# Token-wise sums of squares, a diagonal product that spreads rstd, and a reordered first stage in a fused gMLP, attention and FFN kernel

## The chip, the cores and the metric

The kernel runs on 1 core of one Trainium2 chip. The metric is the device time in microseconds (us) of one execution. Engines are named as the profile names them: PE is TensorE (PEld its weight loads), DVE is VectorE, ACT is ScalarE, POOL is GpSimd, SP is SyncE; a q behind a name is the engine's own instruction stream, which also issues DMAs.

## The reference, cut to what matters

The program computes two blocks on x of 512 tokens by 1024 features: a gated MLP layer, a dilated attention layer with a shared KV projection, then a second block with two SwiGLU layers around a hybrid mixer. The change is in the first layer's start, and in a helper that two later norms use:

```
def ada_mod(c, w, b, n):
    h = jax.nn.silu(c) @ w + b
    return jnp.split(h[:, None, :], n, axis=-1)

def gmlp_layer(...):
    shift, scale, gate = ada_mod(c, ada_w, ada_b, 3)
    h = rms_norm(x, norm_g) * (1 + scale) + shift
    u, v, z = jnp.split(h @ w_in, 3, axis=-1)
    u = jax.nn.gelu(u)
    v = rms_norm(jax.nn.gelu(v), sgu_g)
...
def shared_kv(...):   # and dilated_layer, each with its own shift, scale and norm_g
    shift, scale = ada_mod(c, ada_w, ada_b, 2)
    h = rms_norm(x, norm_g) * (1 + scale) + shift
    k, v = jnp.split(h @ w_kv, 2, axis=-1)
```

rms_norm divides each token by the root of its mean square over the 1024 features; shift and scale are one number per feature. The matrix a_ada_w is 1024 x 3072 (shift, scale, gate), the v part of w_in is 1024 x 2048.

## The kernel before, in words

Activations lie transposed (features on partitions, tokens along the row): `xT` holds 8 tiles (`KD` = 8) of 128 features x 512 tokens. Every large product is made of three passes with operands split into a rounded high part and a low remainder. ACT makes the high part by a copy, DVE the low part by a subtraction. Weights come in chunks of 128 x 2048 numbers into the two slots of `raw` (SP issues the DMAs, `chunk_half` for the v part); `high_part(q, s, ...)` on ACT and `low_part(q, s)` on DVE split slot s of pair q; the low part's end raises `w_ready`, on which PE waits in `chunk` and SP in `wait_slot` before it fills a slot again.

All order is written by hand: each engine runs its own stream, and semaphores tie the streams. The first stage goes as follows.

- SP loads c and x (`xin`, 4 DMAs, token-major), waits for the sixth tile of a_ada_w (`ada0_landed[0]` at 32), then loads the first weight pair, `wsp`, `relrow` and the spatial bias. POOL loads the 8 tiles of a_ada_w (1 MB each, shift and scale columns) into five buffers `ada0_w`; ACT's queue loads 21 small rows (biases and norm gains, tables A and B, and the convolution's taps, `conv_dw_w`, last).
- PE waits for all the rows and transposes them into `sc[0]`, then turns x, 4 transposes for each `xT` tile, and between them sums the squares of finished tiles with a ones matrix into `misc` (`sum_square`), which gives every partition the sum for each token.
- ACT copies each turned tile to `xT` and squares it. DVE adds up c times a_ada_w in `ada0_acc` (`ada0_tile`, one a_ada_w tile at a time, the eighth in halves), with the column copies after the third tile, and `reciprocal_root(0)` (mean square, ACT's root, a reciprocal over 128 x 512) between the sixth and the seventh.
- PE sums `ada0_acc` over partitions (`ada_sum`, 8 one-column products for shift and 8 for scale). DVE adds the bias (`ada_columns`), forms (1 + scale) g (`scale_columns`), and `apply` makes the 8 tiles of h: a multiply by scale and `rstd`, an add of shift, then the low part after ACT's high part (`high_of`).
- `v_block(b)`, b = 0 to 3, multiplies h by 512 columns of v: 8 tiles of h x 4 token blocks x 3 passes = 96 passes of 512 columns, into `v_bank`; the first four tiles use slot 0, the last four slot 1. ACT takes the banks out with Gelu, and `v_block(b + 1)` waits for that. Between blocks 0 and 1 PE transposes `wsp`, which ACT copies to `wsT`.

`apply` runs again after the output product of the layer ("ao"): for the KV norm all eight tiles in one go, and for the attention norm two tiles at a time inside the KV loop (`m` < 4). There the order on DVE is, for each m, `next_low`, `kv_after` (two reciprocals for the k norm), then `apply` of two tiles; ACT's `next_high` for the next chunk stands behind the high parts of those tiles. The loops of "ao" on ACT and DVE are register loops (`Fori`).

## Time and profile before

| | |
|---|---|
| median of 3 runs | 2167.16 us (2163.77 to 2168.45) |
| profiled execution, its own time | 2169.68 us |
| its span | 2168.1 us |
| instructions | 23510 |
| PE busy | 1988.6 us, 92% |
| DVE busy | 1139.0 us, 53% |
| ACT busy | 795.1 us, 37% |
| DMA | 198.40 MB, mean 92 GB/s |

The profiled execution's time is 1.6 us more than its span, and 2.5 us above the median. A busy PE is not a PE at its peak, since the clock granted to it can be 1.2 or 2.4 GHz (0.50 or 1.00 in the profile).

### The profile page before, as it was taken

What the parts mean: (1) busy time and instruction counts of PE and PEld (TensorE: products, weight loads), DVE (VectorE), ACT (ScalarE), POOL (GpSimd) and SP (SyncE); (2) the same over time, 40 slices, a digit from 0 to 9 for tenths busy, and PEclk for the clock granted to TensorE, in tenths of its full rate; (3) what the DMA queues carried; (4) which work ended last, traced back from release to release, by engine and by line L of the source; (5) the groups of instructions that cost most, each with busy time, mean ns of one, the idle gap of its engine ahead of it and who ended that gap; (6) DMA issues with size and microseconds to landing.
All of it is one profiled execution on the core that took longest, in us unless ns stands there. A gap on an engine that the chain in (4) does not pass through costs nothing.

```text
span 2168.1 us, 23510 instructions
## 1 busy us (share of the span) xinstructions
PE 1988.6 (92%) x8658; PEld 1570.8 (72%) x8658; DVE 1139.0 (53%) x1408; ACT 795.1 (37%) x995; POOL 38.6 (2%) x95
## 2 busy tenths in 40 slices
PE   3899999989999999799999996899996989999997
PEld 2688888867777777478888884686664757888885
DVE  4436656468344454454433456399744555433455
ACT  2336554233355444332222233223334343222232
POOL 1000000000000000000000000000000000000000
PEclk9899999979999999899999998999998999999998
DMA  6345555412212121023333322232210223334321
GB/s 256 127 142 158 167 173 164 144 55 75 74 42 59 39 59 39 20 83 96 91 96 101 97 82 73 78 112 64 59 46 32 78 58 97 92 88 112 97 73 63
DMA packets 288193, 198.40 MB, mean 92 GB/s; under 512 B 6562, under 2 KB 275188, under 8 KB 287092
## 3 DMA queue, kind: packets, MB, share of 16 engines
q1 hardware_dynamic: 279568, 163.63, 26.3%
q0 software_dynamic: 8064, 33.56, 4.4%
q8 instruction: 52, 0.85, 0.2%
q10 hardware_dynamic: 484, 0.16, 0.0%
q14 instruction: 25, 0.20, 0.0%
HBM read 195.21 MB, written 2.11 MB: 91 GB/s over the span
## 4 chain that ended last, share of the span: by engine, by line
PE 82%; DVE 10%; ACT 4%; issue 3%; DMA 1%; ACTq 0%; DVEq 0%
PE acc L563 19%; PE acc L565 19%; PE acc L564 19%; PE acc L738 3%; PE acc L740 3%; PE acc L739 3%; PE ob L796 2%; PE sc L755 2%; DVE s_rstd L1426 1%; ACT s_w_high L1004 1%; PE acc L946 1%; PE acc L948 1%; PE acc L947 1%; PE ob L779 1%; DMA s_rows<-in_conv_dw_w 1%
## 5 line engine op out<-in xcount | busy, mean ns | idle before, releaser
L1388 DVE TENSOR_TENSOR s_w_low<-s_raw,s_w_high 128x2048 fp32r<-128x2048 f32 x160 | 366.7, 2292 | 360.4 <-ACT s_w_high L1004 360.1
L563 PE MATMUL acc<-s_h_high,s_w_high 128*128 128x512 f32 x1248 | 492.9, 395 | 32.3 <-DVE s_h_low L1747 12.2
L565 PE MATMUL acc<-s_h_high,s_w_low 128*128 128x512 f32 x1248 | 486.5, 390 | 0.0
L564 PE MATMUL acc<-s_h_low,s_w_high 128*128 128x512 f32 x1248 | 486.5, 390 | 0.0
L1004 ACT ACTIVATE s_w_high<-s_raw 128x2048 fp32r<-128x2048 f32 x160 | 305.1, 1907 | 28.0 <-PE sc L642 19.3
L563 PEld LDWEIGHTS acc<-s_h_high,s_w_high 128*128 128x128 f32 x1248 | 234.8, 188 | 91.5 <-issue 35.2
L563 PE MATMUL acc<-s_b_high,s_w_high 128*128 128x512 f32 x640 | 257.9, 403 | 33.3 <-DVE s_branch L1938 15.9
L565 PEld LDWEIGHTS acc<-s_h_high,s_w_low 128*128 128x128 f32 x1248 | 234.7, 188 | 49.0
L564 PEld LDWEIGHTS acc<-s_h_low,s_w_high 128*128 128x128 f32 x1248 | 235.0, 188 | 48.6 <-issue 1.4
L565 PE MATMUL acc<-s_b_high,s_w_low 128*128 128x512 f32 x640 | 253.5, 396 | 0.0
L564 PE MATMUL acc<-s_b_low,s_w_high 128*128 128x512 f32 x640 | 253.4, 396 | 0.0
L563 PEld LDWEIGHTS acc<-s_b_high,s_w_high 128*128 128x128 f32 x640 | 122.9, 192 | 67.0 <-DVE s_branch L1938 17.6
L564 PEld LDWEIGHTS acc<-s_b_low,s_w_high 128*128 128x128 f32 x640 | 123.2, 193 | 26.0 <-issue 1.0
L565 PEld LDWEIGHTS acc<-s_b_high,s_w_low 128*128 128x128 f32 x640 | 122.7, 192 | 26.2
L1770 DVE TENSOR_TENSOR s_hd<-s_rstd,acc 128x512 f32<-128x512 f32 x44 | 30.2, 687 | 166.4 <-PE acc L565 166.4
L738 PE MATMUL acc<-s_h_high,s_w_high 128*128 128x512 f32 x256 | 113.4, 443 | 0.8 <-DVE s_v L1634 0.8
L1027 ACT ACTIVATE s_b_high<-s_hd 128x512 f32 (+1 forms) x44 | 27.8, 632 | 208.4 <-DVE s_hd L1773 208.4
L740 PE MATMUL acc<-s_h_high,s_w_low 128*128 128x512 f32 x256 | 103.6, 405 | 0.0
L739 PE MATMUL acc<-s_h_low,s_w_high 128*128 128x512 f32 x256 | 103.6, 405 | 0.0
L1839 DVE SCALAR_TENSOR_TENSOR s_cy<-s_glu,s_cols,s_cy 128x512 f32<-128x512 f32 x120 | 81.3, 745 | 0.0
L1240 ACT ACTIVATE s_sg<-s_sg 128x512 f32<-128x512 f32 x44 | 27.8, 632 | 133.8 <-DVE s_sg L1768 133.8
L1684 DVE SCALAR_TENSOR_TENSOR s_s_row<-sc,s_tiny,s_bias 128x256 f32<-128x256 f32 (+3 forms) x96 | 43.7, 511 | 55.7 <-PE sc L755 32.7
(257 smaller groups left out, 2323.5 us busy)
## 6 DMA issues: line engine op xcount, KB each, us to landing
s_raw<-in_a_w_in SPq DMA_DIRECT2D x48, 512.0 KB, 5.0
s_raw<-in_ffn_w_gate SPq DMA_DIRECT2D x44, 512.0 KB, 4.0
s_raw<-in_ffn_w_up SPq DMA_DIRECT2D x44, 512.0 KB, 5.2
s_raw<-in_w_in SPq DMA_DIRECT2D x36, 512.0 KB, 4.4
s_raw<-in_b_w_in SPq DMA_DIRECT2D x32, 512.0 KB, 4.9
s_ada_w<-in_b_ada_w POOLq DMA_DIRECT2D x24, 512.0 KB, 5.0
s_raw<-in_ffn_w_down SPq DMA_DIRECT2D x32, 384.0 KB, 4.2
s_raw<-in_ffn_w_down SPq DMA_DIRECT2D x32, 320.0 KB, 3.7
```

Of the source, the lines that this page charges most:

```text
L563: pe.matmul(acc[b][:, :], w_high[:, o:o + P], hi, start=(k == 0), stop=False, skip_group_check=grouped)
L564: pe.matmul(acc[b][:, :], w_high[:, o:o + P], lo, start=False, stop=False, skip_group_check=grouped)
L565: mm = pe.matmul(acc[b][:, :], w_low[:, o:o + P], hi, start=False, stop=(k == nk - 1), skip_group_check=grouped)
L738: pe.matmul(acc[b][:, :], w_high[:, o:o + P], hi, start=(k == 0), stop=False, skip_group_check=True)
L739: pe.matmul(acc[b][:, :], w_high[:, o:o + P], lo, start=False, stop=False, skip_group_check=True)
L740: mm = pe.matmul(acc[b][:, :], w_low[:, o:o + P], hi, start=False, stop=(k == KD - 1), skip_group_check=True)
L755: mm = pe.matmul(sc[g][:, DIST_W[g] - w:DIST_W[g]], qT[j][g][:, qt * P:(qt + 1) * P], kT[:, k + (qt + 1) * P - w:k + (qt + 1) * P], start= ...
L796: mm = pe.matmul(ob[:, k * P:end * P], v1[:, v:v + P], pT[:, src:src + (end - k) * P], start=(n == 0), stop=(n == len(order) - 1), skip_gr ...
L1004: act.activation(w_high[:, s * SLOT:(s + 1) * SLOT], raw[:, s * SLOT:(s + 1) * SLOT], ACT.Copy)\
L1388: dve.tensor_tensor(w_low[:, w], raw[:, w], w_high[:, w].bitcast(F32), ALU.subtract).then_inc(w_ready, 1)
L1684: ins = dve.scalar_tensor_tensor(out=s_row[b][:, at_:at_ + w], in0=sc[g][:, DIST_W[g] - w:DIST_W[g]], scalar=tiny[:, qr:qr + 1], in1=bias[ ...
L1839: dve.scalar_tensor_tensor(out=cy_n, in0=seg(glu, i + n * GW, T), scalar=col("conv_dw_w_2", i * CT + n), in1=cy_n, op0=ALU.mult, op1=ALU.a ...
```

## The change

The sums of squares of the first norm are no longer made from the turned tiles. ACT squares the token-major `xin` and accumulates along the row, so each token (partition) gets its own sum in a column of `tiny`; the root and the reciprocal are of 128 x 4 numbers. DVE multiplies the identity by these four columns (`diag`, 128 x 512), and one product of a ones matrix with `diag` puts rstd of every token on every partition, in `misc`; `apply` reads it there. PE turns x before it turns any rows, and only table A's rows; table B's and the taps are turned after `v_block(0)`, and `wsp` after `v_block(1)`. DVE runs six a_ada_w tiles in a row. The last tile's halves run scale first, and its sum goes ahead. Twelve products without use (`WARM`) stand on PE behind the sixth a_ada_w tile. The first weight slot is split in quarters, its low parts between the tiles of `apply`, and the second slot's behind the sixth tile. In `apply` with a shift, the add of the shift moves into ACT's high part (Identity with a bias) and into DVE's subtraction; `n2` goes. A Gelu of four numbers stands on ACT ahead of the block loop, and `high_part` of a block's second slot comes ahead of the squares of v. The "ao" loops on ACT and DVE are unrolled. SP's first weights wait for the seventh a_ada_w tile; rows, `wsp` and `relrow` lie elsewhere in memory, and POOL waits for `rel_stored` before its later loads.

```diff
+WARM = 12
...
+        x_sq_out = [at(f"x_sq_out{j}", o, D) for j, o in enumerate((TMP + 2 * TILE, HH))]
+        diag = at("diag", TMP + TILE, T)
         rstd = at("rstd", TMP + TILE, T)
         sq = [at(f"sq{j}", TMP + (2 + j) * TILE, T) for j in range(2)]
         n1 = [at(f"n1{j}", TMP + (4 + j) * TILE, T) for j in range(2)]
-        n2 = [at(f"n2{j}", TMP + (6 + j) * TILE, T) for j in range(2)]
...
-            sp.wait_ge(ada0_landed[0], 32)
+            sp.wait_ge(ada0_landed[1], 32)
...
+            pool.wait_ge(rel_stored, 16)
...
-            pe.wait_ge(rows_landed, 16 * ROW_DMAS)
-            pe.wait_ge(c_ready, 1)
-            for j, n in enumerate(ROW_COUNTS):
-                mm = pe.transpose(sc[0][:, j * P:j * P + n], rows[j][0:n, :], ident[0:n, 0:n])
-            mm.then_inc(rows_turned, 1)
...
-                if k >= 2:
-                    sum_square(0, k - 2)
-            sum_square(0, KD - 2)
-            sum_square(0, KD - 1)
-            for b in range(2):
-                pe.wait_ge(ada0_used, KD + b)
-                ada_sum(ada0_acc, b, b * D)
+            pe.wait_ge(rows_landed, 16 * len(ROWS_A))
+            pe.wait_ge(c_ready, 1)
+            pe.transpose(sc[0][:, 0:ROW_COUNTS[0]], rows[0][0:ROW_COUNTS[0], :], ident[0:ROW_COUNTS[0], 0:ROW_COUNTS[0]])\
+                .then_inc(rows_turned, 1)
+
+            pe.wait_ge(ada0_used, KD - 2)
+            for k in range(WARM):
+                pe.matmul(ob[:, 384:512], ident[:, :], ones[:, :], start=True, stop=True)
+            pe.wait_ge(diag_ready, 1)
+            pe.matmul(misc[:, :], ones[:, :], diag[:, :], start=True, stop=True).then_inc(spread_ready, 1)
+            for b in (1, 0):
+                pe.wait_ge(ada0_used, KD + 1 - b)
+                ada_sum(ada0_acc, b, b * D, (sc[0], ob)[b])
...
-                    chunk(2 * b + half)
+                    if b > 0 or half > 0:
+                        chunk(2 * b + half)
                     for kk in range(4):
                         k = 4 * half + kk
+                        if b == half == 0 and kk < 3:
+                            pe.wait_ge(first_low, kk + 1)
+                        elif b == half == 0:
+                            chunk(0)
...
+            pe.wait_ge(rows_b_landed, 16 * (len(ROWS_B) + 1))
+            pe.wait_ge(cols_ready, 1)
+            for j, n in enumerate(ROW_COUNTS):
+                if j > 0:
+                    mm = pe.transpose(sc[0][:, j * P:j * P + n], rows[j][0:n, :], ident[0:n, 0:n])
+            mm.then_inc(rows_b_turned, 1)
+            v_block(1)
             pe.wait_ge(wsp_ready, 1)
-            pe.wait_ge(cols_ready, 1)
+            pe.wait_ge(cols_b_ready, 1)
...
+                if shift is None:
+                    act.activation(seg(dst, k * T, T), src, ACT.Copy).then_inc(done, 1)
+                else:
+                    act.activation(seg(dst, k * T, T), src, ACT.Identity, bias=shift).then_inc(done, 1)
...
+            act.wait_ge(x_landed, 16 * TT)
             for k in range(KD):
                 act.wait_ge(x_turned, k + 1)
                 act.activation(xT[:, k * T:(k + 1) * T], xb[k % 3][:, :], ACT.Copy).then_inc(x_stored, 1)
-                act.wait_ge(x_stored, k + 1)
-                square(xT[:, k * T:(k + 1) * T], k % 2, 0, k)
-            root(0)
-            high_part(0, 0, 0)
+                if k % 2 == 0:
+                    t = k // 2
+                    if t >= 2:
+                        act.wait_ge(x_sq, t - 1)
+                    act.activation(x_sq_out[t % 2][:, :], xin[:, t * D:(t + 1) * D], ACT.Square,
+                                   accum_out=tiny[:, V_SS + t:V_SS + t + 1]).then_inc(x_sq, 1)
+            act.wait_ge(ms_ready, 1)
+            act.activation(tiny[:, V_RT:V_RT + 4], tiny[:, V_MS:V_MS + 4], ACT.Sqrt).then_inc(root_ready, 1)
+            act.wait_ge(w_landed[0], 32)
+            for k in range(4):
+                act.activation(w_high[:, k * T:(k + 1) * T], raw[:, k * T:(k + 1) * T], ACT.Copy)\
+                   .then_inc(first_high if k < 3 else w_high_ready, 1)
             for k in range(KD):
-                high_of(n2[k % 2][:, :], h_high, k, h32_ready, k + 1, h_high_ready)
+                high_of(n1[k % 2][:, :], h_high, k, h32_ready, k + 1, h_high_ready, shift=ada[:, SHIFT_A + k:SHIFT_A + k + 1])
+                if k == 3:
+                    high_part(0, 1, 0)
+            act.activation(tiny[:, V_MS:V_MS + 4], tiny[:, V_SS:V_SS + 4], ACT.Gelu_apprx_tanh)
             for b in range(4):
-                high_part(b, 1, 4 * b)
                 act.wait_ge(half_used, b + 1)
                 high_part(b + 1, 0, 0)
-                if b == 0:
+                if b == 1:
...
+                if b < 3:
+                    high_part(b + 1, 1, 4 * b + 4)
...
-            with act.Fori(0, 4) as i:
+            for i in range(4):
...
-                high_of(n2[k % 2][:, :], b_high, k, h32_ready, KD + k + 1, h_high_ready)
+                high_of(n1[k % 2][:, :], b_high, k, h32_ready, KD + k + 1, h_high_ready,
+                        shift=ada[:, SHIFT_KV + k:SHIFT_KV + k + 1])
...
+            def apply(hbase, scale, shift, high, low, tiles=range(KD), spread=None, between=None):
+
+                def low_tile(k):
+
+                    dve.wait_ge(h_high_ready, hbase + k + 1)
+                    low_k, high_k = low[:, k * T:(k + 1) * T], high[:, k * T:(k + 1) * T].bitcast(F32)
+                    if shift is None:
+                        dve.tensor_tensor(low_k, n1[k % 2][:, :], high_k, ALU.subtract).then_inc(h_ready, 1)
+                    else:
+                        dve.scalar_tensor_tensor(out=low_k, in0=n1[k % 2][:, :], scalar=shift(k), in1=high_k,
+                                                 op0=ALU.add, op1=ALU.subtract).then_inc(h_ready, 1)
 
                 for k in tiles:
-                    if k >= 2:
+                    if hbase + k >= 2:
                         dve.wait_ge(h_high_ready, hbase + k - 1)
                         dve.wait_ge(h_ready, hbase + k - 1)
-                    x_k = xT[:, k * T:(k + 1) * T]
-                    if shift is None:
-                        dve.scalar_tensor_tensor(out=n2[k % 2][:, :], in0=x_k, scalar=scale(k), in1=rstd[:, :],
-                                                 op0=ALU.mult, op1=ALU.mult).then_inc(h32_ready, 1)
-                    else:
-                        own.done(dve.scalar_tensor_tensor(out=n1[k % 2][:, :], in0=x_k, scalar=scale(k), in1=rstd[:, :],
-                                                          op0=ALU.mult, op1=ALU.mult))
-                        dve.tensor_scalar(n2[k % 2][:, :], n1[k % 2][:, :], shift(k), None, ALU.add).then_inc(h32_ready, 1)
+                    dve.scalar_tensor_tensor(out=n1[k % 2][:, :], in0=xT[:, k * T:(k + 1) * T], scalar=scale(k),
+                                             in1=(rstd if spread is None else spread)[:, :],
+                                             op0=ALU.mult, op1=ALU.mult).then_inc(h32_ready, 1)
+                    if between is not None:
+                        between(k)
                     if k > tiles[0]:
-                        low_of(n2[(k - 1) % 2][:, :], high, low, k - 1, h_high_ready, hbase + k, h_ready)
-                k = tiles[-1]
-                low_of(n2[k % 2][:, :], high, low, k, h_high_ready, hbase + k + 1, h_ready)
-
-            def ada_columns(n0, n1_, read):
+                        low_tile(k - 1)
+                low_tile(tiles[-1])
...
-            for k in range(3):
+            for k in range(6):
                 ada0_tile(k)
+            dve.wait_ge(x_sq, TT)
+            dve.tensor_scalar(tiny[:, V_MS:V_MS + 4], tiny[:, V_SS:V_SS + 4], 1.0 / D, EPS, ALU.mult, ALU.add).then_inc(ms_ready, 1)
+            ada0_tile(6)
+            dve.wait_ge(root_ready, 1)
+            dve.reciprocal(tiny[:, V_R:V_R + 4], tiny[:, V_RT:V_RT + 4]).then_inc(x_rcp, 1)
+            dve.wait_ge(x_rcp, 1)
+            dve.tensor_tensor(diag[:, :].rearrange("p (t q) -> p t q", t=TT),
+                              ident[:, None, :].broadcast_to([P, TT, P]),
+                              tiny[:, V_R:V_R + 4].rearrange("p (t q) -> p t q", q=1).broadcast_to([P, TT, P]),
+                              ALU.mult).then_inc(diag_ready, 1)
             dve.wait_ge(rows_turned, 1)
-            for j, n in enumerate(ROW_COUNTS):
-                ins = dve.tensor_copy(cols[:, j * P:j * P + n], sc[0][:, j * P:j * P + n])
-            ins.then_inc(cols_ready, 1)
+            dve.tensor_copy(cols[:, 0:ROW_COUNTS[0]], sc[0][:, 0:ROW_COUNTS[0]]).then_inc(cols_ready, 1)
             dve.wait_ge(cols_ready, 1)
-
+            for half in (1, 0):
+                ada0_tile(7, half)
+            ada_columns(8, 16, 1)
+            dve.wait_ge(ada_cols, 1)
+            scale_columns(A_A, SHIFT_A + KD, "a_norm_g")
+            ada_columns(0, 8, 2, sc[0])
+            dve.wait_ge(ada_cols, 2)
+            dve.wait_ge(spread_ready, 1)
+
+            def first_lows(k):
+
+                if k < 4:
+                    part = slice(k * T, (k + 1) * T)
+                    if k < 3:
+                        dve.wait_ge(first_high, k + 1)
+                    else:
+                        dve.wait_ge(w_high_ready, 1)
+                    dve.tensor_tensor(w_low[:, part], raw[:, part], w_high[:, part].bitcast(F32), ALU.subtract)\
+                       .then_inc(first_low if k < 3 else w_ready, 1)
+                elif k == 5:
+                    low_part(0, 1)
+
+            apply(0, lambda k: derived_col(A_A + k), lambda k: ada_col(SHIFT_A + k), h_high, h_low,
+                  spread=misc, between=first_lows)
...
-            for k in range(3, 6):
-                ada0_tile(k)
-            reciprocal_root(0)
-            ada0_tile(6)
-            for half in range(2):
-                ada0_tile(7, half)
-            low_part(0, 0)
-            ada_columns(0, 16, 2)
-            dve.wait_ge(ada_cols, 1)
-            scale_columns(A_A, SHIFT_A + KD, "a_norm_g")
-            apply(0, lambda k: derived_col(A_A + k), lambda k: ada_col(SHIFT_A + k), h_high, h_low)
...
+                if b == 0:
+                    dve.wait_ge(rows_b_turned, 1)
+                    for j, n in enumerate(ROW_COUNTS):
+                        if j > 0:
+                            ins = dve.tensor_copy(cols[:, j * P:j * P + n], sc[0][:, j * P:j * P + n])
+                    ins.then_inc(cols_b_ready, 1)
+                    dve.wait_ge(cols_b_ready, 1)
+                    for dst, name in ((HG1, "ffn1_norm_post_2"), (HG2, "ffn2_norm_post_2")):```

The order is shown at three places. First DVE, from its first instruction to the first tile of `apply`. Before (`s_ada_acc` is `ada0_acc`, `s_ada_w_77` to `81` its five buffers):

```order
L1474 SCALAR_TENSOR_TENSOR s_ada_acc<-s_ada_w_79,s_tiny,s_ada_acc 128x2048
L1481 COPY s_cols<-sc 128x106
L1481 COPY s_cols<-sc 128x84
L1481 COPY s_cols<-sc 128x124
L1485 SCALAR_TENSOR_TENSOR s_derived<-s_cols 128x1
L1488 TENSOR_SCALAR s_derived<-s_cols 128x8 x2
L1474 SCALAR_TENSOR_TENSOR s_ada_acc<-s_ada_w_80,s_tiny,s_ada_acc 128x2048
L1474 SCALAR_TENSOR_TENSOR s_ada_acc<-s_ada_w_81,s_tiny,s_ada_acc 128x2048
L1474 SCALAR_TENSOR_TENSOR s_ada_acc<-s_ada_w_77,s_tiny,s_ada_acc 128x2048
L1418 TENSOR_SCALAR s_n_68<-misc 128x512
L1426 RECIPROCAL s_rstd<-s_n_69 128x512
L1474 SCALAR_TENSOR_TENSOR s_ada_acc<-s_ada_w_78,s_tiny,s_ada_acc 128x2048
```

Of the change, the same stretch on DVE, from the sixth a_ada_w tile to the first tile of `apply`:

```order
L1519 SCALAR_TENSOR_TENSOR s_ada_acc<-s_ada_w_78,s_tiny,s_ada_acc 128x2048
L1525 TENSOR_SCALAR s_tiny<-s_tiny 128x4
L1519 SCALAR_TENSOR_TENSOR s_ada_acc<-s_ada_w_79,s_tiny,s_ada_acc 128x2048
L1528 RECIPROCAL s_tiny<-s_tiny 128x4
L1530 TENSOR_TENSOR s_diag<-s_ident,s_tiny 128x512
L1535 COPY s_cols<-sc 128x106
L1519 SCALAR_TENSOR_TENSOR s_ada_acc<-s_ada_w_80,s_tiny,s_ada_acc 128x1024 x2
L1495 TENSOR_TENSOR s_ada<-ob,s_cols 128x8
L1498 SCALAR_TENSOR_TENSOR s_derived<-s_ada,s_cols 128x8
L1495 TENSOR_TENSOR s_ada<-sc,s_cols 128x8
L1483 SCALAR_TENSOR_TENSOR s_n_71<-s_xT,s_derived,misc 128x512
```

The copy of the columns stands behind the seventh tile instead of the third, and the reciprocal is of 4 columns. Second, PE of the change around the end of `v_block(0)` (L651, L653 and L655 are its passes, `s_rows_86` and `87` the late rows):

```order
L651 MATMUL sc<-s_w_high,s_h_high 128x512
L653 MATMUL sc<-s_w_low,s_h_high 128x512
L655 MATMUL sc<-s_w_high,s_h_low 128x512
L667 MATMUL sc<-s_ident,s_rows_86 128x84
L667 MATMUL sc<-s_ident,s_rows_87 128x124
L651 MATMUL acc<-s_w_high,s_h_high 128x512
```

Where these two transposes stand there were eight of `wsp` before (L653 of the kernel before). Third, ACT of the change, from the last high part of h to the second block's copies of `wsT`:

```order
L1050 ACTIVATE s_h_high<-s_n_72,s_ada 128x512
L1089 ACT_TABLE_LOAD
L1089 ACTIVATE s_tiny<-s_tiny 128x4
L1024 ACTIVATE s_w_high<-s_raw 128x2048
L1100 ACTIVATE s_v_tok<-acc 128x4x128 x2
L1100 ACTIVATE s_v_tok<-sc 128x4x128 x2
L1024 ACTIVATE s_w_high<-s_raw 128x2048
L1109 ACTIVATE s_sq_69,s_tiny<-s_v_tok 128x512
```

The Gelu's table load stands ahead of block 0's end; before, it stood behind the copies of `wsT`, directly ahead of the first Gelu. POOL gains one wait, and SP's DMAs keep their order.

## Rows read from the trace of the kernel before

**Rows 1.** The page: engine shares (part 1) and two groups of part 5.

```profile
PE 1988.6 (92%) x8658; PEld 1570.8 (72%) x8658; DVE 1139.0 (53%) x1408; ACT 795.1 (37%) x995; POOL 38.6 (2%) x95
...
L1388 DVE TENSOR_TENSOR s_w_low<-s_raw,s_w_high 128x2048 fp32r<-128x2048 f32 x160 | 366.7, 2292 | 360.4 <-ACT s_w_high L1004 360.1
```

**Rows 2.** The chain that ended last, 0 to 110 us: start, us, what.

```profile
8.85 20.04 DMA s_rows<-in_conv_dw_w
...
43.90 3.36 DVE s_rstd L1426
47.29 2.36 DVE s_ada_acc L1474
...
51.09 7.00 PE ob L596 x32
58.52 0.76 DVE s_n L1439
59.31 0.49 DVE s_n L1441
```

**Rows 3.** Timeline at 25 us: start, us, engine and line, [idle before <-releaser].

```profile
25.60 1.92 SPq L358 DMA_DIRECT2D s_raw<-in_a_w_in  x4
```

**Rows 4.** DMA issues in windows at 3.0, 12, 17 and 26 us: KB, us to landing.

```profile
s_xin<-in_x SPq DMA_DIRECT2D x1, 512.0 KB, 12.3
...
s_ada_w<-in_a_ada_w POOLq DMA_DIRECT2D x1, 1024.0 KB, 13.0
...
s_ada_w<-in_a_ada_w POOLq DMA_DIRECT2D x1, 1024.0 KB, 11.3
...
s_raw<-in_a_w_in SPq DMA_DIRECT2D x1, 512.0 KB, 7.6
```

**Rows 5.** Windows: us, busy PE, PEld, DVE, ACT, POOL, then PEclk, DMA share, GB/s.

```profile
61.70:74.30 12.60, 12.58 (x48) 9.98 (x48) 11.70 (x19) 4.58 (x7) 0.00 (x0) 0.88 0.01 2
77.69:90.34 12.65, 12.65 (x49) 10.20 (x49) 2.36 (x2) 1.92 (x1) 0.00 (x0) 0.87 0.55 178
458.30:471.50 13.20, 11.25 (x21) 6.16 (x22) 11.79 (x20) 5.16 (x7) 0.00 (x0) 0.50 0.00 1
1370.00:1374.00 4.00, 2.34 (x11) 1.65 (x10) 1.36 (x2) 2.49 (x2) 0.00 (x0) 1.00 0.85 230
1374.00:1377.00 3.00, 3.00 (x15) 2.47 (x14) 1.68 (x1) 0.00 (x0) 0.00 (x0) 1.00 0.05 10
```

**Rows 6.** Timeline of 61 to 120 us, blocks 0 and 1 of v.

```profile
61.72 0.77 PE L638 MATMUL acc<-s_w_high,s_h_high 128*128 128x512 f32 x1 [3.65 <-DVE s_h_low L1399]
...
77.69 0.50 PE L638 MATMUL acc<-s_w_high,s_h_high 128*128 128x512 f32 x1 [3.38 <-DVE s_w_low L1388]
...
78.51 33.63 SPq L358 DMA_DIRECT2D s_raw<-in_a_w_in  x9
...
92.51 1.28 ACT L1065 ACT_TABLE_LOAD   x1
...
94.55 0.47 PE L638 MATMUL acc<-s_w_high,s_h_high 128*128 128x512 f32 x1 [3.17 <-ACT s_v_tok L1065]
...
118.01 0.39 PE L638 MATMUL acc<-s_w_high,s_h_high 128*128 128x512 f32 x1
```

**Rows 7.** Timeline of PE at 161 us: one ada_sum of 8 columns.

```profile
161.53 1.84 PE L596 MATMUL ob<-s_ones,s_gate_acc 128*128 128x1 f32 x16
163.24 0.49 PE L563 MATMUL acc<-s_h_high,s_w_high 128*128 128x512 f32 x1
```

**Rows 8.** Timeline of 455 to 510 us: KV norm and KV loop.

```profile
455.13 0.75 DVE L1439 SCALAR_TENSOR_TENSOR s_n<-s_xT,s_derived,s_rstd 128x512 f32<-128x512 f32 x1
...
470.11 0.80 PE L563 MATMUL acc<-s_b_high,s_w_high 128*128 128x512 f32 x1 [0.33 <-DVE s_b_low L1399]
...
497.57 0.63 ACT L1027 ACTIVATE s_h_high<-s_n 128x512 fp32r<-128x512 f32 x1 [0.55 <-DVE s_n L1441]
...
509.09 0.76 PE L563 MATMUL acc<-s_b_high,s_w_high 128*128 128x512 f32 x1 [3.72 <-ACT s_k_sq L1113]
```

70 lines of the change are left out of this document (38 added, 32 removed).

## The prediction, made before the changed kernel ran

> **What bounds the kernel now.** I read the engine shares first: PE is busy for 92% of the span, DVE for 53% [rows 1]. A change that takes nothing off PE's products can only win where PE stands still or runs at its lower clock. So I went to the chain of the first 110 us, where PE's first large product starts only at 61.72 [rows 6]. Its first long link is a DMA: the taps of the convolution are issued at 8.85 and land 20.04 us later, and PE, which waits for all rows, turns nothing until 28.9 [rows 2]. The x that it could have turned landed at about 2.8 + 12.3 = 15.1 [rows 4]. Behind that the chain goes through turning x and summing squares to 42.5, the reciprocal over 128 x 512 (3.36), the seventh and eighth a_ada_w tiles and the one-column sums (7.00), until `apply` starts at 58.52 [rows 2]. The timeline then shows two more holes in PE: 3.38 us ahead of the second half of block 0, where the low part of slot 1 stands behind all eight tiles of h, and 3.17 ahead of block 1, behind the copies of `wsT`, a table load and the first Gelu [rows 6]. After each hole some passes run at 1.2 GHz: 48 passes took 12.6 us in both halves of block 0 at a mean granted clock of 0.88 and 0.87 [rows 5]. At full clock a pass takes 0.227 (the timeline's pitch; 96 passes from 94.55 to 118.01 are 23.46, less the passes at half clock below), so 48 are 10.9 and each ramp costs 1.7. Later, the KV norm feeds PE tile by tile from 455.13 to 470.11 [rows 8].
>
> **A. From the start to `apply`.** The waits for rows and for squares go; what is left is the pace of a_ada_w. Tile 6 is issued behind the first tile's use at 12.6 and lands at 12.6 + 13.0 = 25.6, when SP, waiting for it, issues its weights [rows 3, 4]. Each tile on DVE takes 2.36 [rows 2]: 28.0. The mean square of 128 x 4 is a small operation of about 0.2 (two of them lie between the end of the sums at 58.09 and 58.52 [rows 2]): 28.2. Tile 7 lands at 17.3 + 11.3 = 28.6 [rows 4] and is done at 30.9. The small reciprocal 0.2, `diag` 0.7 (DVE's operations on 512 columns cost 0.49 to 0.76 [rows 2]), the column copy 0.2: 32.0. Two halves at 1.3: 33.3 and 34.6. The scale sum runs from 33.3; eight columns take 1.71 at full clock [rows 7] and 3.5 at half (7.00 for sixteen [rows 2]). At full clock the two sums end at 35.0 and 36.8, and with the last small operations `apply` starts at 37.3 against 58.52: **21.2 us**. At half clock it is 40.9 and 17.6. [...]
>
> What lies beside it: ACT copies and squares x from 16 on, eight copies of 0.6 and four squares of 1024 columns, each half of a 2048-column copy (1.9) plus 0.2 for the accumulator, some 10 us, ended at 26; it is covered by DVE's tiles until 28.0. Without that cover each us counts in full. SP's first weights are issued at 28.6 instead of 25.6; the first slot then took until 26.1 + 7.6 = 33.7 [rows 4], now 36.7 at most. ACT's first quarter is ready at 37.4, DVE asks for it at 38.0. This is the thinnest cover: 0.6 us.
>
> **B. `apply` and block 0.** A tile had a period of 1.97 on DVE: 0.79 for the multiply, 0.40 for the shift, 0.78 for the low part. Now it is the multiply (reading rstd from PSUM, which I bound by the same 0.75, since the multiply-add of the residual reads PSUM at that price) and a low part of 0.75: 1.46. Four quarters of a low part add 0.6 each (2292 ns over four [rows 1]). The first tile is ready after two multiplies, two quarters and its low part, 3.3 us; before it was 3.2: **-0.1**. With quarters a tile takes 2.1, less than PE's 2.7 for twelve passes at full clock, so PE is not starved again. The low part of slot 1 is then done 11.8 us into `apply`, PE asks at 3.3 + 12.6 = 15.9: the hole of 3.38 goes, and with it the second ramp, 1.7: **5.1**.
>
> **C. Block 0 to block 1.** Block 0 ended at 90.34, block 1 began at 94.55, 4.21 later [rows 5, 6]. Now two short transposes, 0.3, and the Gelu of the first bank has its 2 us before the block ends: **3.9**, and no ramp in block 1: **1.7**. But the weights of block 1 must be there. DVE ends `apply` 16.3 after its start, then the small operations, 0.4, SP's next issue 0.7, 5.4 until landing (78.51 to 83.87), ACT 1.95, DVE 2.3: 27.1. PE is through with block 0 at 3.3 + 12.6 + 10.9 + 0.3 = 27.1. A tie; I charge nothing and keep 1 us for the range.
>
> **D. Block 1 to block 2.** The transposes of `wsp` move here: 1.0 for them, 1.1 for the two copies, 0.65 for the Gelu, 0.1 of waits: **-2.9**. PE is idle for 1.8 of it. A hole of 1.66 at 1370 us is like this (PE busy for 2.34 of 4.00), and the clock stayed at 1.00 in and behind it [rows 5], so I add no ramp (it would be 1.7).
> The load that B and C take from the path is priced by its row, 1.28, with the Gelu following at 93.81 [rows 6]. The Trainium skill, "ScalarE: Activation LUTs", What ACT_TABLE_LOAD costs, gives some 1.38 us of drain on top; by it the gain would be 1.4 more, 2133.1 on the runs' scale, inside the forecast's own range. The trace shows no such drain on this load.
>
> **E. The two later norms.** The KV norm's last tile was ready 14.95 after its first multiply (470.11 against 455.13 [rows 8]). At 1.46 a tile it is 11.8: **3.1**. In the KV loop the two high parts stand ahead of the weight's high part on ACT; the second began at 497.57 [rows 8], after the multiply and the shift of its tile. Without the shift it follows the first directly, 0.6 earlier, once before PE's hole of 3.72 at 509.09 [rows 8], behind which PE is busy: **0.6**. Unrolling the "ao" loops: 0.2 at the last tile's register waits, else hidden by PE.
>
> **Other edits at nothing:** table B's columns and the halved gains are made while DVE waits in block 1; the second slots' high parts go ahead of squares that nobody needs until block 3's end; POOL's new wait ends near 57, and its next loads wait for uses long after. Without these covers each is 0.2 to 2 us.
>
> **Sum:** 21.2 - 0.1 + 5.1 + 3.9 + 1.7 - 2.9 + 3.1 + 0.6 + 0.2 = 32.8. The v, "uz" and "ao" stages between are PE-bound without holes (none is listed from 118 to 446), so it is passed on. The profiled 2169.7 becomes 2136.9; the runs' median is 2.5 lower, so **2134.5**, I say 2135.
>
> **The rivals.**
> 1. *The sums run at 1.2 GHz, or the weights are late* (0.14). For it: the 32 one-column passes at 51 us ran at half clock to their end, 7.00 against twice 1.71 [rows 2, 7], and the cover of 0.6 at the first quarter is thin. Against: dense products go right ahead. 3.6 less, with a late quarter or a ramp in D of 1.7 more: 2138 to 2142.
> 2. *The gain of B and C comes back as a wait for weights* (0.05). If SP's second pair lands late, behind `wsp`, the spatial bias and POOL's four gate tiles, block 1 waits as it did: 10.6 less, 2145.
> 3. *PE is starved tile by tile and never gets its clock* (0.02). In the KV norm PE ran 13.2 us at 0.50 because each tile came alone, PE busy for 11.25 of it [rows 5]. If an operand in PSUM made a tile of `apply` dearer than PE's 2.7, block 0 would run at half clock, and if that lasted over 33 / 0.2 = 165 passes the gain would be gone; over all four blocks, 384 passes, it is 77 - 33 = 44 slower: 2211. Against: 2.1 is well under 2.7, and after block 0 h is all there.
> 4. *It does nothing* (0.01): if a_ada_w's tiles came later by what the rows were earlier. Against: their DMAs are issued by the same uses as before, 2167.
> 5. *More than the sum* (0.08): PE, fed every 1.46 with 1.28 of work at half clock, may get its clock inside the KV norm, 24 passes earlier at 0.2, some 2 to 5: 2130 to 2133.
>
> **How the numbers follow.** My forecast (0.70) is 2135 with 2131 to 2139 as its own range: half clock in one sum, 1 us in C, 1.7 in D, and the KV loop's other two savings of 0.6. Rival 5 reaches down to 2130; I take 2128, since the squares of x and the small operations are not in the trace. Upwards rival 1 reaches to 2142, and I take 2144 for both of its parts with a wait in C. That leaves out rivals 2 to 4 and a tenth beside. A measurement of this kernel tells 0.2%, some 4.3 us, from no change. Faster: all but rivals 3 and 4, 0.97; the same 0.01; slower 0.02.
>
> **What would show it.** In the changed kernel: PE's first transposes of x near 15 to 16; the last a_ada_w half ended near 34.6; each ada_sum 1.7 long; the first multiply of `apply` near 37 and PE's first pass of v near 41; no hole between the halves of block 0; a hole under 1 us ahead of block 1 and one of about 1.8 ahead of block 2, which starts near 89; the KV norm's tile period 1.46. Wrong would make it: ada_sums of 3.5, a first quarter that DVE waits for, a period over 2.7 in `apply`, or a later stage that has a new hole.

## The result, and the profile of the changed kernel

The changed kernel takes 2128.71 us (median of 4 runs, 2128.28 to 2132.92), the kernel before 2167.8 on the same chip (4 runs, 2163.77 to 2170.78). The ratio is 0.9834 with a 95% interval of 0.9820 to 0.9847: 1.5 to 1.8% faster. The medians differ by 39.1 us, the spans of the two profiled executions by 2168.1 - 2127.1 = 41.0. The forecast was 2135 with a gain of 32.8.

The page's engine shares answer to [rows 1]:

```profile
PE 1971.6 (93%) x8668; PEld 1563.1 (73%) x8668; DVE 1125.9 (53%) x1389; ACT 796.2 (37%) x999; POOL 38.8 (2%) x95
```

The chain that ended last (start, us, what) answers to [rows 2]:

```profile
12.65 12.95 DMA s_ada_w<-in_a_ada_w
25.62 2.36 DVE s_ada_acc L1519
28.02 5.26 PE ob L624 x24
33.28 0.86 PE misc L626 x2
34.15 1.68 PE ob L603 x16
35.83 2.85 PE sc L603 x16
38.97 0.75 DVE s_n L1483
```

The DMA of the taps is gone from the chain; the pace of a_ada_w is on it, as forecast. But what follows the sixth tile is not DVE's last two tiles. It is PE's own `WARM` products, 5.26 long, and the `diag` product and the two sums stand in line behind them. `apply` starts at 38.97, before at 58.52.

The timeline of all engines from 31 to 43 us shows both sides of that, and what came behind it (start, us, engine, line, [idle before <-releaser]):

```profile
31.86 2.48 DVE L1519 SCALAR_TENSOR_TENSOR s_ada_acc<-s_ada_w,s_tiny,s_ada_acc 128x1024 f32<-128x1024 f32 x2
...
33.98 1.84 PE L603 MATMUL ob<-s_ones,s_ada_acc 128*128 128x1 f32 x16
35.69 2.98 PE L603 MATMUL sc<-s_ones,s_ada_acc 128*128 128x1 f32 x16
...
39.96 1.32 POOL L508 TENSOR_SCALAR_AFFINE_SELECT s_wsp<-s_wsp 128x1024 f32<-128x1024 f32 x1 [19.44 <-DMA s_wsp<-in_a_w_spatial]
...
40.90 0.92 DVE L1554 TENSOR_TENSOR s_w_low<-s_raw,s_w_high 128x512 fp32r<-128x512 f32 x1
...
42.63 0.77 PE L651 MATMUL acc<-s_w_high,s_h_high 128*128 128x512 f32 x1 [3.96 <-DVE s_h_low L1476]
```

DVE ended at 34.34, within 0.3 of the forecast. The first sum ran in 1.84, the second needed 2.98. A low part of a weight quarter took 0.92 where its neighbours take 0.68, in the very microsecond in which POOL masks `wsp`.

Windows (us, busy PE, PEld, DVE, ACT, POOL, PEclk, DMA share, GB/s) show the granted clock in that stretch, and below it the stretches of block 0, block 1 and the KV norm; they answer to [rows 5]:

```profile
30.00:32.00 2.00, 2.00 (x11) 2.00 (x11) 1.93 (x5) 0.00 (x0) 0.00 (x0) 0.50 0.91 326
...
34.00:35.00 1.00, 1.00 (x11) 1.00 (x10) 0.34 (x1) 1.00 (x3) 0.00 (x0) 1.00 0.91 301
...
37.00:38.00 1.00, 1.00 (x6) 1.00 (x6) 0.00 (x0) 0.00 (x0) 0.00 (x0) 0.50 1.16 355
...
42.63:66.36 23.73, 23.73 (x96) 19.40 (x97) 15.09 (x19) 11.13 (x13) 0.71 (x2) 0.92 0.49 178
66.70:88.30 21.60, 21.60 (x97) 17.85 (x96) 7.32 (x8) 6.62 (x11) 1.06 (x2) 1.00 0.57 195
...
433.00:435.00 2.00, 2.00 (x5) 1.22 (x5) 1.90 (x3) 0.72 (x1) 0.00 (x0) 0.50 0.00 0
435.00:437.00 2.00, 1.89 (x6) 0.81 (x4) 1.90 (x4) 0.96 (x2) 0.00 (x0) 0.83 0.00 0
437.00:440.00 3.00, 1.93 (x6) 0.97 (x6) 2.79 (x5) 1.41 (x3) 0.00 (x0) 1.00 0.00 0
```

PE was busy without a gap from 30 to 38, yet its clock was at 1.2 GHz, then 2.4, then 1.2 again. Block 0 is one piece now, 96 passes in 23.73 (before 28.62 from 61.72 to 90.34), with one ramp; block 1 has none. In the KV norm the clock comes back at about 435.7; before it stayed at 0.50 to the end of that stretch.

The timeline of PE at two later places answers to [rows 6, 8]:

```profile
91.18 0.47 PE L651 MATMUL acc<-s_w_high,s_h_high 128*128 128x512 f32 x1 [1.75 <-ACT s_v_tok L1100]
...
477.09 0.77 PE L570 MATMUL acc<-s_b_high,s_w_high 128*128 128x512 f32 x1 [3.08 <-ACT s_k_sq L1151]
```

Block 2 starts 26.8 us earlier than before (118.01) and the hole in the KV loop is 0.64 shorter (3.72).

**Where the 41.0 us come from.** I paired PE's instructions of the two traces and read by how much each starts earlier: 26.8 at block 2, 27.1 at the sum of squares ahead of the KV norm, 32.7 at the pass that stood at 535.69, 34.4 at the first scores, 38.4 at the first product of "bo", 40.9 at the end. So some 8 us appear in places that the change does not touch. The experiments below show what these are, as far as they do.

### The profile page after: what moved, and what is told of

It is laid out like the page before. It is cut to its first block, busy times and chain, and to the rows that moved or that the text cites. A ratio compares the mean times of both kernels' runs of the same rounds, so it can differ in the third digit from the quotient of the medians.

```text
span 2127.1 us, 23436 instructions
## 1 busy us (share of the span) xinstructions
PE 1971.6 (93%) x8668; PEld 1563.1 (73%) x8668; DVE 1125.9 (53%) x1389; ACT 796.2 (37%) x999; POOL 38.8 (2%) x95
## 4 chain that ended last, share of the span: by engine, by line
PE 84%; DVE 8%; ACT 4%; issue 3%; DMA 1%; DVEq 0%; POOL 0%; ACTq 0%; POOLq 0%
PE acc L570 20%; PE acc L571 19%; PE acc L572 19%; PE acc L758 3%; PE acc L760 3%; PE acc L759 3%; PE ob L816 2%; PE sc L775 2%; DVE s_rstd L1465 1%; PE acc L966 1%; DMA s_ada_w<-in_a_ada_w 1%; ACT s_w_high L1024 1%; PE ob L799 1%; PE acc L968 1%; PE acc L967 1%
## 5 line engine op out<-in xcount | busy, mean ns | idle before, releaser
L1427 DVE TENSOR_TENSOR s_w_low<-s_raw,s_w_high 128x2048 fp32r<-128x2048 f32 x159 | 364.5, 2292 | 354.0 <-ACT s_w_high L1024 354.0
L570 PE MATMUL acc<-s_h_high,s_w_high 128*128 128x512 f32 x1248 | 494.0, 396 | 31.5 <-DVE s_h_low L1820 11.5
L1024 ACT ACTIVATE s_w_high<-s_raw 128x2048 fp32r<-128x2048 f32 x159 | 303.3, 1907 | 23.7 <-PE sc L655 18.0
L570 PEld LDWEIGHTS acc<-s_h_high,s_w_high 128*128 128x128 f32 x1248 | 235.0, 188 | 89.8 <-issue 36.2
L570 PE MATMUL acc<-s_b_high,s_w_high 128*128 128x512 f32 x640 | 255.9, 400 | 30.4 <-DVE s_branch L2011 15.4
L570 PEld LDWEIGHTS acc<-s_b_high,s_w_high 128*128 128x128 f32 x640 | 121.9, 190 | 62.8 <-DVE s_branch L2011 17.4
## 6 DMA issues: line engine op xcount, KB each, us to landing
s_raw<-in_a_w_in SPq DMA_DIRECT2D x48, 512.0 KB, 5.1
s_raw<-in_ffn_w_gate SPq DMA_DIRECT2D x44, 512.0 KB, 4.0
s_raw<-in_ffn_w_up SPq DMA_DIRECT2D x44, 512.0 KB, 5.2
s_raw<-in_w_in SPq DMA_DIRECT2D x36, 512.0 KB, 4.2
s_raw<-in_b_w_in SPq DMA_DIRECT2D x32, 512.0 KB, 4.9
s_ada_w<-in_b_ada_w POOLq DMA_DIRECT2D x24, 512.0 KB, 5.0
```

Of the source, the lines that this page charges most:

```text
L570: pe.matmul(acc[b][:, :], w_high[:, o:o + P], hi, start=(k == 0), stop=False, skip_group_check=grouped)
L1024: act.activation(w_high[:, s * SLOT:(s + 1) * SLOT], raw[:, s * SLOT:(s + 1) * SLOT], ACT.Copy)\
L1427: dve.tensor_tensor(w_low[:, w], raw[:, w], w_high[:, w].bitcast(F32), ALU.subtract).then_inc(w_ready, 1)
```

## Both kernels again

> The kernel before, again, for its spread. In the first profiles the changed kernel ran 55 passes of 512 columns at half clock outside the parts that the change touches, the kernel before 75, and 8.3 us of the 41.0 between the two profiles stand there. Theory P (the clock's dips fall by chance in time): this second profile of the same code shows another number of slow passes, 55 to 90, and places in the attention stage that moved; the total lies within 2163 to 2172. Rival C (the change carries it): the same dips at the same places, 75 again within 3.

> The changed kernel, again. Theory P: its slow passes outside the touched parts vary too, 50 to 85, and the gain at the start of the third v block stays 26.8 within 0.5, while the gain at the end differs from 40.9 by some us. Rival C: 55 within 3 and 40.9 within 1.

The kernel before took 2166.74 (10 runs) beside 2165.74 of its reference runs, ratio 1.0006 (0.9996 to 1.0015), span 2163.6. The changed kernel took 2132.04 (4 runs, 2128.79 to 2132.98), ratio 0.9849 (0.9825 to 0.9873), span 2127.1: 33.7 by these medians.

By these second profiles the gain at the end is 2163.6 - 2127.1 = 36.5 in place of 41.0, as theory P has it. One thing that I expected did not come: the gain at block 2 did not stay within 0.5 of 26.8. It is 27.4 (117.71 against 90.31), because `apply` started 1.6 earlier in this profile of the changed kernel than in the first.

Windows over two stretches tell the four profiled executions apart: from the sum ahead of the KV norm to the first scores, and the attention stage (to "bo"). First the kernel before, its first profile:

```profile
449.20:579.00 129.80, 116.85 (x474) 90.31 (x475) 86.73 (x91) 46.63 (x63) 4.49 (x7) 0.88 0.22 65
579.00:916.80 337.80, 310.73 (x1430) 237.53 (x1428) 161.72 (x294) 159.32 (x257) 0.00 (x0) 0.95 0.16 44
```

Its second profile:

```profile
449.00:579.00 130.00, 117.89 (x474) 91.35 (x475) 86.74 (x91) 45.95 (x63) 4.49 (x7) 0.87 0.23 65
579.00:912.80 333.80, 306.87 (x1430) 234.54 (x1428) 161.43 (x294) 159.67 (x256) 0.00 (x0) 0.96 0.16 45
```

The changed kernel:

```profile
422.10:544.70 122.60, 112.09 (x475) 87.37 (x476) 79.94 (x75) 47.12 (x63) 4.44 (x7) 0.93 0.24 69
544.70:878.30 333.60, 306.42 (x1429) 234.44 (x1427) 161.57 (x294) 159.69 (x257) 0.00 (x0) 0.96 0.16 45
```

The attention stage of one and the same kernel took 337.8 and 333.8. The 4 us are PE's own busy time, 310.7 against 306.9 for the same 1430 records, at a lower mean clock. The changed kernel has 333.7 in both profiles. So 4.1 of the 41.0 is how the clock fell in the first profile of before, and not the change.

The first stretch, up to each profile's own first score, took 129.8 and 130.3 in the two profiles of before, 122.6 and 121.5 in those of the changed kernel: 7 to 9 us less, where I had forecast 3.9. Not all of it is the change's. These are the last 8 us ahead of the first scores, in the kernel before, in the changed kernel, and in the changed kernel with its copies of `wsT` moved, an edit far from this stage (`e12_wst_timed`, below):

```profile
571.00:579.00 8.00, 8.00 (x33) 6.62 (x34) 1.35 (x3) 4.39 (x7) 0.00 (x0) 0.79 0.50 133
...
536.70:544.70 8.00, 8.00 (x48) 7.02 (x48) 2.69 (x3) 4.20 (x8) 0.00 (x0) 1.00 0.49 132
...
535.40:543.40 8.00, 8.00 (x34) 6.59 (x34) 1.29 (x3) 4.06 (x7) 0.00 (x0) 0.79 0.48 131
```

PE is busy throughout in all three, but in the first and the third the clock is lower, and there the work from the pass that stood at 535.69 to the first scores takes 43.2 to 43.3, in the changed kernel 41.6. That is 1.6 us. This dip stands in six of all fourteen profiles, three of them of variants of the changed kernel. Over the ten profiles of the changed kernel and its variants the whole stretch took 121.5 to 124.5, so it gained 5.3 to 8.8.

## The two parts apart: the fold of the shift, and the order of the first stage

The fold alone, on the kernel before:

```diff
-high_of(n2[k % 2][:, :], h_high, k, h32_ready, k + 1, h_high_ready)
+high_of(n1[k % 2][:, :], h_high, k, h32_ready, k + 1, h_high_ready, shift=ada[:, SHIFT_A + k:SHIFT_A + k + 1])
...
+                        dve.scalar_tensor_tensor(out=low_k, in0=n1[k % 2][:, :], scalar=shift(k), in1=high_k,
+                                                 op0=ALU.add, op1=ALU.subtract).then_inc(h_ready, 1)
```

> The kernel before with one part of the change alone: the shift folded into ACT's high part and DVE's subtraction, in all three norms with a shift. My theory: the tile period in the KV norm falls from 1.97 to 1.52 (3.2 over the eight tiles), the KV loop gives 0.7, and the first apply ends 3 us earlier, which lets the second half of block 0 start 3 earlier: 6 to 7 in all, and up to 3 more if the clock comes back inside the KV norm: 2158 to 2162. Rival: the part matters only in the KV stage, where it gave 5.5 in the changed kernel's profile, clock included: 2162 to 2164.

The order alone, on the kernel before (ones-matrix sums of squares kept, x turned ahead of the rows, the column copies behind the eighth tile):

```diff
             for k in range(KD):   # x turned, squares summed
...
             sum_square(0, KD - 1)
+            pe.wait_ge(rows_landed, 16 * ROW_DMAS)
+            pe.wait_ge(c_ready, 1)
+            for j, n in enumerate(ROW_COUNTS):
+                mm = pe.transpose(sc[0][:, j * P:j * P + n], rows[j][0:n, :], ident[0:n, 0:n])
+            mm.then_inc(rows_turned, 1)
```

> The kernel before with the order alone changed: x turned and squared ahead of the rows, DVE's column copies behind the eighth a_ada_w tile; the sums of squares by turned tiles, the reciprocal over 128 x 512 and the rest stay. My theory: the first apply starts at 28.0 + 4.8 (mean square, root, reciprocal) + 2 x 2.4 + 1.2 + 7.0 behind the eighth tile's first half, near 44 to 45, 14 earlier than 58.5, and the time is 2153 to 2155. Rival: the wait for the taps was nearly all of it and the cheaper root is a trifle: 19 to 20 earlier, 2148.

The fold alone took 2152.69 (5 runs, 2149.85 to 2156.68), ratio 0.9949 (0.9928 to 0.9969). That is 13.1 below its reference of 2165.74, and more than I expected. Its timeline of PE:

```profile
60.42 0.77 PE L637 MATMUL acc<-s_w_high,s_h_high 128*128 128x512 f32 x1 [2.89 <-DVE s_h_low L1441]
...
89.38 0.47 PE L637 MATMUL acc<-s_w_high,s_h_high 128*128 128x512 f32 x1 [3.17 <-ACT s_v_tok L1067]
```

Block 0's first pass is 1.3 earlier and block 1 is 5.2 earlier than in [rows 6], with no hole inside block 0: eight tiles at 0.5 less each bring the low part of slot 1 forward by 4, which is more than the 3.38 that PE waited for it. Of the 5.2, 0.5 is that `apply` itself happened to start earlier, at 57.98. The rest of the gain comes later: its stretch from the sum to the first scores took 120.8, before 129.8 and 130.3, so that gain needs none of the other edits.

The order alone took 2150.24 (5 runs, 2147.06 to 2153.95), ratio 0.9931 (0.9909 to 0.9953), 15.5 below the reference and somewhat below the 2153 to 2155 that I expected. Its timelines, of DVE and PE:

```profile
43.94 0.75 DVE L1439 SCALAR_TENSOR_TENSOR s_n<-s_xT,s_derived,s_rstd 128x512 f32<-128x512 f32 x1
...
63.12 0.50 PE L638 MATMUL acc<-s_w_high,s_h_high 128*128 128x512 f32 x1 [2.64 <-DVE s_w_low L1388]
```

`apply` starts 14.6 earlier, the holes remain, and the KV stretch takes 130.4 as before. So of the 19.6 to 21.1 us ahead of `apply`, 14.6 come from not waiting for the rows. The other 5 to 6.5 belong to the rest of the change: the token-wise sums with the small root, the scale sum ahead, and the warming products. Of these only the warming products were tried by themselves (below). The gains of the two parts, 13.1 and 15.5, add up to 28.6, most of the 33.7; a kernel with both and nothing else was not run.

## The warming products

```diff
-WARM = 12
+WARM = 0
```

(In the second kernel `+WARM = 8`; these products have no use in the result.)

> The changed kernel without the twelve products that have no use. Theory W (they raise the clock, but stand in the way): without them the diag product runs at half clock as soon as diag is ready, 31.7 to 33.4, both column sums run at half clock, 3.5 each, and the first apply starts near 40.8 instead of 38.97, 1.8 later. Rival: the products only delay, the sums' speed comes from the turning of x: apply starts near 37.3, 1.7 earlier.

> The changed kernel with eight of these products instead of twelve. In the changed kernel they took 5.26 us at half clock, and the diag product, ready to start at 31.6, started at 33.1. Theory W: with eight they end at 31.5, the diag product is done by 33.4, the sums start with the first half of the last tile at 33.2, at full clock, and apply starts at 37.3 to 38.0, 1.0 to 1.7 earlier. Rival: with less dense work the clock does not rise and apply starts near 40.8, as without any.

Without them, 2136.89 in one run. Its timeline of PE:

```profile
31.86 2.05 PE L626 MATMUL misc<-s_diag,s_ones 128*128 128x512 f32 x2 [9.20 <-DVE s_diag L1530]
33.70 3.41 PE L603 MATMUL ob<-s_ones,s_ada_acc 128*128 128x1 f32 x16
36.97 3.55 PE L603 MATMUL sc<-s_ones,s_ada_acc 128*128 128x1 f32 x16
```

Both sums run at half clock, `apply` starts at 40.83, as worked out for the rival. With eight, 2128.45:

```profile
28.04 3.78 PE L624 MATMUL ob<-s_ones,s_ident 128*128 128x128 f32 x16 [5.93 <-DVE s_ada_acc L1519]
31.80 1.53 PE L626 MATMUL misc<-s_diag,s_ones 128*128 128x512 f32 x2
33.30 1.95 PE L603 MATMUL ob<-s_ones,s_ada_acc 128*128 128x1 f32 x16
35.10 2.70 PE L603 MATMUL sc<-s_ones,s_ada_acc 128*128 128x1 f32 x16
```

Here `diag` is waited for, not PE, and the scale sum starts at 33.30, when DVE has it ready; `apply` starts at 38.11. In the changed kernel's second profile the clock rose sooner, the twelve products took 4.29, the two sums 1.95 and 1.93, and `apply` started at 37.40. So the products bring the start of `apply` forward by 1.9 to 3.4 us, against a single profile without them, and block 2, which stands at 93.15 there, by 2.0 to 2.8. In six profiles with twelve of them that can be compared `apply` started between 37.24 and 38.97, in three with eight between 37.78 and 38.11: twelve cost some of their gain again when the clock rises late. Whether and where the clock falls again inside the second sum differs from run to run. At block 2 hardly anything of the difference was left in this run (91.08 against 91.18), in part because a low part of a weight quarter took 1.50 beside POOL's masking.

## The masking of the spatial weights

In the changed kernel's second profile the low part of the first tile of h took 1.58 instead of 0.74, while POOL masked `wsp`. Theory: the two operations get in each other's way. The experiment puts the masking behind `apply`:

```diff
-            pool.wait_ge(wsp_landed, 16)
-            pool.affine_select(out=wsp[:, :].rearrange("t (g s) -> t g s", g=AG),
...
             for k in range(KD):
+                if k == 4:
+                    pool.wait_ge(h_ready, KD)
+                    pool.wait_ge(wsp_landed, 16)
+                    pool.affine_select(out=wsp[:, :].rearrange("t (g s) -> t g s", g=AG),
```

> The changed kernel with POOL's masking of wsp moved behind the first four gate loads and behind the end of apply. In the changed kernel it ran at 39.96 for 1.32 us, inside apply, and one operation of DVE on 512 columns took 0.92 there instead of 0.68; in the second run of it one took 1.58 instead of 0.74, with eight warm products one took 1.50 instead of 0.68. Theory G (the masking on POOL stretches what DVE does at the same time): no operation in apply is stretched, and PE's first pass of v stands 3.4 us behind apply's first multiply, as in the run without warm products (3.41), not 3.66 to 4.24. Rival: the stretch comes from the loads that land then, or from reading PSUM, and stays.

In one run 2132.3. Its timeline:

```profile
40.70 0.69 DVE L1555 TENSOR_TENSOR s_w_low<-s_raw,s_w_high 128x512 fp32r<-128x512 f32 x1
...
42.19 0.76 PE L652 MATMUL acc<-s_w_high,s_h_high 128*128 128x512 f32 x1 [3.73 <-DVE s_h_low L1477]
...
55.49 1.09 POOL L512 TENSOR_SCALAR_AFFINE_SELECT s_wsp<-s_wsp 128x1024 f32<-128x1024 f32 x1 [18.88 <-DVE s_h_low L1477]
```

No operation of DVE inside `apply` is long any more, and the first pass comes 3.42 behind the first multiply (38.77), against 3.66 and 4.24 in the changed kernel's two profiles. The theory holds. But the masking only met another operation of DVE: the copy that pads the table `relrow` and raises `rel_padded`, behind which SP issues the weights of block 1. It took 0.22 in the changed kernel. The two timelines of DVE, first of the changed kernel, then of this one:

```profile
55.96 0.22 DVE L1579 COPY s_relrow<-s_relrow 8x127 f32<-8x127 f32 x1
...
55.52 1.13 DVE L1580 COPY s_relrow<-s_relrow 8x127 f32<-8x127 f32 x1
```

It ended 0.07 behind POOL's end. The weights went out 0.9 later by it, and a hole of 0.55 appeared ahead of block 1. That, and an attention stage of 337.4, is why the whole was not faster.

## The copies of wsT, and the split of slot 1

The copies behind block 1's Gelus and the next high part:

```diff
                 if b < 3:
                     high_part(b + 1, 1, 4 * b + 4)
+                if b == 1:
+                    act.wait_ge(wsp_turned, 1)
+                    act.activation(wsT[:, 0:512], sc[0][:, :], ACT.Copy)
+                    act.activation(wsT[:, 512:1024], tr[0][:, :], ACT.Copy).then_inc(wsT_ready, 1)
```

> The changed kernel with ACT's two copies of wsT behind the second block's Gelus and the next high part instead of ahead of them. My theory: the Gelus of block 1 then run as its banks finish, PE's hole of 1.75 ahead of block 2 goes, and block 2 starts 0.9 to 1.1 after block 1's end instead of 2.79: 1.7 to 1.9 earlier. Rival: the hole stays, because PE waits in it for the weights of slot 0.

In one run 2126.02. Its timeline of PE:

```profile
89.03 0.60 PE L673 MATMUL tr<-s_ident,s_wsp 128*128 128x128 f32 x4
89.39 0.48 PE L651 MATMUL acc<-s_w_high,s_h_high 128*128 128x512 f32 x1
```

The hole of 1.75 is gone and block 2 starts 1.8 earlier than in the changed kernel: 1.8 of the 2.9 of term D of the forecast was the copies' place on ACT, and needn't be paid. Timed:

> The changed kernel with the copies of wsT moved behind block 1's Gelus, now timed. The single look had 2126.0 us and block 2 1.8 us earlier than the change. Theory: those 1.8 us are kept to the end, so the median lies 1.0 to 2.5 below the change's, 2126 to 2129. Rival: what is won there is within the spread that the attention stage and the others bring, so the median lies between 2129 and 2133, and the two can't be told apart. The hole ahead of block 2 is gone in both.

2127.43 (5 runs, 2124.6 to 2128.65), ratio 0.9824 (0.9809 to 0.9838), against 0.9834 and 0.9849 of the changed kernel. The median is where the theory put it, but the intervals overlap, so a gain over the changed kernel is likely and not shown. Its stretch from the sum to the first scores took 124.5, with the dip of the clock that was shown above, against 121.5 in the single run before it.

The low part of slot 1 behind all eight tiles, as in the kernel before:

```diff
-                elif k == 5:
-                    low_part(0, 1)
...
                   spread=misc, between=first_lows)
+            low_part(0, 1)
```

> The changed kernel with the split of slot 1 back behind all eight tiles of h, on ACT and DVE. My theory: the hole between the halves of block 0 is back, near 3.4 (54.6 for the last high part, 1.9 and 2.3 for the split, 58.8, against PE at 55.2), with 1.7 for the clock's ramp: block 1 starts 5 later than 66.7. Rival: with the shorter apply the hole is under 1.5 and the clock stays, under 1.5 in all.

In one run 2132.51, with PE's hole at

```profile
57.37 0.50 PE L651 MATMUL acc<-s_w_high,s_h_high 128*128 128x512 f32 x1 [1.41 <-DVE s_w_low L1426]
```

The hole is 1.41, not 3.38, there is no second ramp, and block 2 starts 2.0 later than in the changed kernel, where my term B would have it 5 later. So on the kernel before the fold alone closes the hole. In the changed kernel, whose `apply` also carries the four quarters of slot 0, the fold leaves 1.41 of it, which the moved split closes. The moved split without the fold was not run.

## The repairs together

Eight warming products, the late masking and the late copies in one kernel:

> The changed kernel with eight warm products, the masking of wsp behind apply, and the copies of wsT behind the second block's Gelus. My theory: apply starts at 37.3 to 38.2, PE's first pass is 3.4 later, no hole ahead of block 2, which starts 2.5 to 3.5 earlier than 91.18, near 88; the time is 2124 to 2127. Rival: the weights of block 1 (a load that is issued only behind the end of apply) take back what is won ahead of it, a hole of 0.5 to 1.5 stands there, and only the 1.7 ahead of block 2 stays: 2126 to 2129.

2130.59 (5 runs, 2130.04 to 2134.53), ratio 0.9843 (0.9830 to 0.9856), longer than both ranges that I had named. Block 2 starts at 88.71, 2.5 earlier than in the changed kernel, and yet the whole is not faster. The timelines of SP and PE show a longer wait ahead of block 1:

```profile
55.73 0.29 SPq L411 DMA_DIRECT2D rel_ext<-s_relrow  x1
56.44 26.15 SPq L364 DMA_DIRECT2D s_raw<-in_a_w_in  x10
...
66.02 0.50 PE L652 MATMUL acc<-s_w_high,s_h_high 128*128 128x512 f32 x1 [1.10 <-DVE s_w_low L1428]
```

SP's queue stands at its wait for `rel_padded`, which DVE raises behind `apply`, and the weights of block 1 stand behind it. The copy that raises it ran beside the late masking here too and took 1.14 in place of 0.22, so some 0.9 of the 1.10 is again the masking, by my estimate from these two durations. The rest of what is missing is its attention stage, which took 337.4. Whether that is chance is open: with 333.7 this kernel would take some 2126.3 by my estimate (2130.04 less 3.7), and none of its five runs was under 2130.04. The last kernel lets SP issue these weights first:

```diff
-            sp.wait_ge(rel_padded, 1)
-            sp.dma_start(rel_ext, relrow[:, :]).then_inc(rel_stored, 16)
-
             with sp.Fori(1, 4) as i:
                 for s in range(2):
                     chunk_half(i, s, W["a_in"], i * 512 + AW)
+            sp.wait_ge(rel_padded, 1)
+            sp.dma_start(rel_ext, relrow[:, :]).then_inc(rel_stored, 16)
```

> This is the last kernel (8 warming products, the masking of the spatial weights late, the copies of wsT behind the Gelus) with one more edit: SP issues the weights of the blocks 1 to 3 ahead of its wait for rel_padded and its store of the padded table, not behind them. Theory: the hole of 1.10 us ahead of block 1 in the last run was SP's queue, which stood at that wait until the end of apply and issued the block-1 weights only at 56.4. Then here the weights land before PE asks for them, the hole is gone (under 0.2), and block 2 starts 0.9 to 1.1 earlier, at 87.6 to 87.8. Rival: the weights wait for their slots, which block 0 frees, and land no earlier; then the hole stays at 1.0 to 1.2 and block 2 at 88.7. On the whole time: the stretch up to the accsq sum should be 121.5 to 122.5 less 1, and the attention stage either 333.7 or 337.4 as in the runs before, so 2122 to 2128 in the first case, 2126 to 2131 in the second. If the attention stage is at 337.4 again, as in the two other kernels with the late masking, the theory that its length is chance loses weight against one in which the earlier start itself decides it.

2124.14 (5 runs, 2123.81 to 2132.66), ratio 0.9819 (0.9799 to 0.9839), the lowest median of all, with an interval that reaches into the changed kernel's. Its timelines of SP and PE:

```profile
44.81 37.29 SPq L364 DMA_DIRECT2D s_raw<-in_a_w_in  x10
...
65.55 0.48 PE L651 MATMUL acc<-s_w_high,s_h_high 128*128 128x512 f32 x1
```

The weights are issued from 44.81 on, not from 56.44, and the hole is gone. Block 2 starts at 88.22, only 0.5 earlier than in the kernel before it and later than the 87.6 to 87.8 that I expected. Block 0 took 24.4 in place of 23.6 at a mean clock of 0.90 in place of 0.93, which gave most of the 1.1 back. The copy took 1.13 here as well, but the weights no longer stand behind it. Its attention stage took 333.9 with the same late masking, so the late masking does not by itself decide that stage's length.

Over all fourteen profiles the attention stage took 333.6 to 333.9 in ten (one of them of the kernel before), 336.1 once and 337.4 to 337.8 in three (one of them of the kernel before), with no edit that goes with either. The two of the changed kernel's variants at 337.4 both have the late masking, and so has one at 333.9: too few to tell.

## Why the prediction was right, and where its terms were off

1. **What bounds the kernel, and A's mechanism: right.** PE's transposes of x start at 14.95 (said: 15 to 16) and the last a_ada_w half ends at 34.34 (34.6). The order alone shows the wait for the rows to be 14.6 of it.
2. **A's size: 19.6 in the first profile, 21.1 in the second; said 21.2.** The step that failed in the first profile is that both sums were put at full clock, and that the products ahead of them were charged nothing. The twelve products took 5.26 us in the first profile and 4.29 in the second, at half clock for all or most of it, so they held the `diag` product back (33.12, where `diag` was ready at 31.6), and in the first profile the clock fell within the second sum: 2.98 in place of 1.71. It was full clock in one sum, not in both (in the second profile in both, 1.95 and 1.93); without the products it was neither, 40.83 as rival 1 had it. The quarter of weights, my thinnest cover, was not waited for.
3. **B: the first pass was said to come 3.3 behind the first multiply and came 3.66 and 4.24 behind it.** I named only the weights as a danger there, and missed POOL's masking, which the earlier start of `apply` brought to lie beside it (it starts when `wsp` has landed, at 39.96 and 39.76). With it moved away the distance is 3.42.
4. **B, C and D as a sum: right.** From the first multiply to block 2 it took 59.49 before and 52.21 in the changed kernel (52.91 in its second profile), 7.3 and 6.6 less; the terms give -0.1 + 5.1 + 3.9 + 1.7 - 2.9 = 7.7. The hole and the ramp in block 0 went, block 1 had no ramp, the hole ahead of block 2 was 1.75 (said: 1.8). The table load stands at 55.08 now, takes 1.28, and the Gelu behind it starts 0.02 after its end (56.38): the drain on top that the Trainium skill, "ScalarE: Activation LUTs", What ACT_TABLE_LOAD costs, puts on a load is not seen here either. But the 5.1 was put down to the moved split alone, and two experiments show that on the kernel before the fold by itself removes that hole, and that in the changed kernel only 1.41 of it comes back without the moved split.
5. **C's tie: it was one.** The weights were just in time in the first profile. In the second (`apply` from 37.40) block 1 waited 0.28 for them, and 0.55 and 1.10 in the two kernels in which the late masking held back SP's queue. In the other variants there was no such wait, even with `apply` from 37.24. I kept 1 us in the range for it.
6. **E: said 3.9, measured 7.2 and 8.3, the term that was sized too small.** A tile's period fell from 1.98 to 1.52 (said 1.46). The pass that stood at 470.11 came 14.98 behind the first multiply before and comes 11.51 behind it now: 3.5, where 3.1 was said. The hole in the KV loop fell by 0.64 (said 0.6). What was missing is rival 5's: PE got its clock back inside the KV norm, at about 435.7, when a tile came every 1.52. The passes of 512 columns at half clock around that norm fell from 27 and 26 to 8 and 8, and the gain grew from 26.9 at the first of its passes to 31.3 at the 28th. I gave this 8%, and it came in all eleven profiles with the fold, and in none of the three without: from the sum to the 28th pass it is 24.9 in those three and 19.8 to 20.8 in the eleven. With the 0.64 of the hole that makes 4.8 to 5.7, which every kernel with the fold has. The other 2.5 of the gain is more full clock behind the norm. 1.6 of it is the dip ahead of the first scores, which three variants of the changed kernel have as the kernel before has it, so it isn't shown to be the change's.
7. **The other rivals.** No sum of the changed kernel ran wholly at half clock; PE was fed every 2.1 in block 0 and had its clock from 46.4 on (rival 3 did not come); the wait for the weights of block 1 never passed 1.10 (rival 2).
8. **The median: in part luck.** The sum with the measured terms is 19.6 + 7.3 + 7.2 = 34.1 in the first profile and 21.1 + 6.6 + 8.3 = 36.0 in the second, between the two measured differences of 33.7 and 39.1. The profiled difference of 41.0 holds 4.1 of chance in the attention stage and up to 2.5 in the stages behind it (1246.8 and 1246.1 before, 1244.3 and 1246.2 after), which no forecast from one profile could hold. The forecast of 32.8 lies near these sums because its errors have opposite signs: in the first profile A was put 1.6 too high and E 3.3 too low. The median of 2128.71 lies below the forecast's own range of 2131 to 2139 and close to the 2128 that was taken for rival 5; the 2132.04 of the second comparison lies inside the own range. What decides where the clock dips in the untouched stages is open.

## What to carry to other kernels

When a stage is started earlier, look at everything that now lies beside it: another engine's operation that used to be harmless, and a queue whose next DMA waits for the end of the stage. The same holds for a repair: the masking, moved out of `apply`, met the one small copy on which that queue waited. Count a product that only keeps the clock up as work on its engine, as long as it stands ahead of something that is waited for. And where an engine is fed piece by piece, a shorter piece is worth more than its own saving if it lets the clock come back: price that as a case of its own.

## What the runs showed of the hardware

**DVE and POOL blocked each other.** The masking (128 x 1024, in place) takes 1.09 alone. In six profiles it overlapped an operation of DVE that reads two tensors from SBUF and started after it, and each of these ended 0.54 or 0.55 behind POOL's end, whenever it had started: 41.28 and 41.82 in the changed kernel, 40.96 and 41.50 in its second profile, and 41.00 and 41.54, 41.21 and 41.76, 40.34 and 40.89, 40.81 and 41.35 with eight products, the late copies, the late split and the late copies timed. The multiply of `apply`, with one operand in SBUF and one in PSUM, ran inside the masking at 0.74 as ever. Where DVE's operation had started first, POOL's took up to 1.63, and ended 0.95 or 0.96 behind DVE's end. These two rows of the changed kernel's second profile show the pair:

```profile
39.76 1.20 POOL L508 TENSOR_SCALAR_AFFINE_SELECT s_wsp<-s_wsp 128x1024 f32<-128x1024 f32 x1 [19.16 <-DMA s_wsp<-in_a_w_spatial]
39.92 1.58 DVE L1476 SCALAR_TENSOR_TENSOR s_h_low<-s_n,s_ada,s_h_high 128x512 fp32r<-128x512 f32 x1
```

The Trainium skill, "SBUF — State Buffer", Who interferes with whom, says that a DVE instruction with two SBUF inputs contends with a GpSimd instruction that reads SBUF, and that one with at most one such input does not, outside the 2-port modes, which a copy can enter; and that the order of issue decides who blocks. The traces agree: besides the rows above, the copy of 8 x 127, with a single SBUF input, took 1.13 or 1.14 in place of 0.22 in the three kernels with the late masking, and ended 0.07 behind POOL's end. That this copy ran in such a mode is not shown by any run.

**A busy PE did not hold its clock.** The one-column products of the sums kept PE busy for every slice from 34 to 38 us, and the granted clock fell from 1.00 to 0.50 within them; without warming products it never rose in the 6.8 us that both sums took. In two other profiles, with twelve products, it stayed at 1.00 through both sums (1.84 to 1.95 each).

**An Identity with a bias** on 128 x 512 takes ACT 0.72, the Copy that it replaced 0.63. It did not show here: in the KV norm a tile's period is 1.52, and DVE is busy for 1.49 of it.
